# Two-branch decoder layer on one core: compression of keys and values with four products for three output chunks, and the next unit's pages turned inside both halves of the products

## The chip, the cores and the metric

One core of one Trainium2 chip runs the whole kernel as a single program. The metric is the time of one execution on the device in microseconds (us). All data is float32.

## What is computed

The reference is one inference step of a decoder layer for a prompt of 1024 tokens and for 8 decode sequences with 2048 past tokens each. The change touches one stage of it, the compression of the raw keys and values of the past into compressed blocks:

```python
def _compress(kraw, w1, b1, w2, b2, pe):          # CMP_STRIDE = 16, CMP_LEN = 32, CMP_RATIO = 2, CMP_HIDDEN = 256
    ch = kp.reshape(B, n_ch, CMP_STRIDE, NSA_KV_HEADS, HEAD_DIM)
    w1r = w1.reshape(CMP_RATIO, CMP_STRIDE, HEAD_DIM, CMP_HIDDEN)
    parts = jnp.einsum('bnsgd,rsdh->rbngh', ch, w1r)
    n_cmp = n_ch - CMP_RATIO + 1
    h = parts[0, :, 0:n_cmp] + parts[1, :, 1:1 + n_cmp]
    h = h + (pe.reshape(-1) @ w1) + b1
    return jax.nn.gelu(h) @ w2 + b2
```

A sequence of 2048 tokens has 128 chunks of 16 tokens. Output n needs chunk n times the first half of w1 and chunk n + 1 times the second half, so each of the 127 outputs of a sequence and a group of heads is h[n] = A x[n] + B x[n+1], with A and B of 1024 rows (8 tiles of 128) and 256 columns (two halves of 128). It is done for keys and for values, for the prompt (64 chunks) and for 8 sequences, with 2 groups of heads.

## The kernel before

The stage is `compress_and_decode`. The projections of the prompt run ahead of it, the attention of the decode tokens and of the prompt behind it.

**Units and items.** There are NU = 10 units: unit 0 (keys of the prompt), units 1 to 4 (keys of two sequences each), unit 5 (values of the prompt), units 6 to 9 (values of two sequences each). A prompt unit has one item, the others two, one for each sequence. `loads` is the ring of four 1 MB page buffers (`raw0` to `raw3`) that GpSimd fills by indirect DMA in `load`.

**Turning.** `transposes` turns an item's 16 pieces of 128x128 on TensorE into four PSUM banks, by turns in banks 0 to 2 of PS, so a bank can be written when the bank three before it has been read (`bank_free`). ScalarE reads the even banks and VectorE the odd ones (`read_chunks`, with `copy` at L1163), two copies of 64 partitions x 512 for each bank, and puts even and odd chunks apart in the buffer X, which has room for two units.

**Products.** For a pair of outputs the kernel computes three products instead of four: with e and o the even and odd chunks, A (e - o), B (e' - o) and (A + B) o, where e' is the even chunk that follows. The sum A + B is `w1_sum`. GpSimd makes e' - o (`later_difference`, L991), then VectorE makes e - o in place (`first_difference`, L1258). `layer1` runs the products: for each half hh of the hidden columns, 8 matmuls of 256 columns (L1070), 8 of 252 (L1072), and 8 of 256 (L1077). In the trace every one of these float32 matmuls is two weight loads and two MATMUL records. The products of the prompt units are 63 to 65 columns wide.

**Behind the products.** ScalarE copies the shared product to `middle` (L1213), VectorE adds it to the two others (`sums`, L1274 and L1275), ScalarE applies the GELU, and TensorE multiplies with w2 a unit later (`layer2`, L1090 and L1095). Each of the 8 sequence units also does a piece of the layer's modulation: `late_rows` (L1042) multiplies 512 columns of w_ada, ScalarE copies them (L1219), `late_back` (L1049) turns them, and VectorE adds the result to adaT (`late`, L1299) and raises `wa_added`, for which the next `late_rows` waits. The 2 MB of each piece of w_ada are loaded by SyncE once the piece before it is used. In units 1 and 6 `late_rows` stands ahead of the second half, in the others ahead of the first.

**Order of the work.** It is written out by hand. Each engine has one in-order queue, and semaphores join them. TensorE's loop is:

```python
            for u in range(NU):
                if u + 1 < NU:
                    for k in units[u + 1][2]:
                        transposes(pe, items[k])
                layer1(u)
                if u:
                    layer2(u - 1)
                if u in late_at:
                    late_back(late_at.index(u))
```

`layer1(u)` waits for all differences of its unit, then for the `sums` of the same half of unit u - 1. VectorE reads the odd banks of a unit's items, makes the two `first_difference`, and does then `sums` of the unit before. GpSimd, behind the item of unit 5, waits for the end of the products of unit 4 and makes the sum of the value weights (L1004), then goes on with unit 6.

## Time and profile before

| | |
|---|---|
| median of 3 runs | 2244.59 us (2244.12 to 2252.13) |
| the profiled execution, its own time | 2242.59 us |
| its span in the trace | 2240.8 us |
| mean granted TensorE clock, of full speed | 0.978 |
| TensorE busy | 2122.5 us, 95% of the span |
| VectorE, ScalarE, GpSimd busy | 50%, 35%, 40% |
| the stage of the change | from 183.9 us to 452 us of the span |

The span is what the profiler saw between the first and the last instruction, and the execution's own time is 1.8 us longer. PE is TensorE's matmuls, PEld its weight loads, DVE VectorE, ACT ScalarE, POOL GpSimd. Times of rows are counted from the start of the span.

### The profile page before, as it was taken

The numbers are of one execution on the slowest core, as the hardware profiler recorded it, in microseconds if no ns is written. First come the engines' busy times: TensorE is split into PE (matmuls) and PEld (weight loads), VectorE is DVE, ScalarE is ACT, GpSimd is POOL, SyncE is SP. The second block draws the span as 40 slices with busy tenths as digits, with TensorE's granted clock in tenths as the row PEclk, the third lists the DMA queues.
The fourth block names the chain that finished last, engine by engine and source line by source line (L and its number), as shares of the span: only waits on it lengthen the run. The fifth ranks groups of instructions, "written<-read, shape, count | busy, mean of one in ns | idle before, by whom it ended". The sixth has DMA issues, their size and how long they took to land. (4 is left out here: it accounts for less than half of the span.)

```text
span 2240.8 us, 37919 instructions
## 1 busy us (share of the span) xinstructions
PE 2122.5 (95%) x15414; PEld 1875.2 (84%) x15414; DVE 1115.9 (50%) x2002; ACT 791.1 (35%) x1594; POOL 893.2 (40%) x620
## 2 busy tenths in 40 slices
PE   5998999999999989997899999899999999999998
PEld 3997787855777689987799999678999999997886
DVE  5114323254766720259631045666876665664558
ACT  3203222134566621336522131234333333333553
POOL 2322222120111231212321124164388788776786
PEclk8999999998999999998999999999999999999999
DMA  7564434274110051100223130221245344357872
GB/s 265 195 219 153 178 119 150 87 277 167 32 32 11 1 142 38 38 8 3 69 67 95 38 113 20 100 88 65 71 148 178 123 146 165 123 183 272 272 230 104
DMA packets 152757, 268.20 MB, mean 120 GB/s; under 512 B 17817, under 2 KB 86348, under 8 KB 147975
## 3 DMA queue, kind: packets, MB, share of 16 engines
q1 hardware_dynamic: 144375, 222.70, 29.8%
q0 software_dynamic: 8208, 43.07, 5.5%
q8 instruction: 123, 2.02, 0.4%
q14 instruction: 51, 0.41, 0.1%
HBM read 211.93 MB, written 58.08 MB: 120 GB/s over the span
## 5 line engine op out<-in xcount | busy, mean ns | idle before, releaser
L3448 PE MATMUL PS<-down_parts 128*128 128x512 f32 x924 | 213.3, 392 | 0.1
L3448 PEld LDWEIGHTS PS<-down_parts 128*128 128x128 f32 x924 | 174.2, 189 | 38.0 <-issue 0.9
L3405 PE MATMUL PS<-part_hi,w_ring 128*128 128x258 f32 x1152 | 192.2, 285 | 0.0
L3405 PEld LDWEIGHTS PS<-part_hi,w_ring 128*128 128x128 f32 x1152 | 161.8, 191 | 4.6 <-issue 4.6
L3405 PE MATMUL PS<-sum_blocks,w_ring 128*128 128x258 f32 x1296 | 160.1, 284 | 0.9 <-DVE out_sums L3971 0.9
L3405 PEld LDWEIGHTS PS<-sum_blocks,w_ring 128*128 128x128 f32 x1296 | 158.3, 190 | 1.2 <-DVE out_sums L3971 1.2
L643 POOL TENSOR_TENSOR w_merge_parts<-w_merge_raw,w_merge_parts 128x1024 fp32r<-128x1024 f32 x24 | 59.5, 2503 | 202.5 <-ACT w_merge_parts L636 202.5
L3797 POOL TENSOR_TENSOR down_parts<-down_raw,down_parts 128x512 fp32r<-128x512 f32 x71 | 117.4, 1667 | 45.6 <-ACT down_parts L3603 45.2
L2343 PE MATMUL PS<-h_hi,w_merge_parts 128*128 128x344 f32 x768 | 131.4, 323 | 0.0
L2343 PEld LDWEIGHTS PS<-h_hi,w_merge_parts 128*128 128x128 f32 x768 | 122.0, 188 | 3.1 <-issue 3.0
L1809 ACT ACTIVATE scores<-scores,mins_p 128x640 f32<-128x640 f32 (+5 forms) x192 | 112.4, 588 | 28.0 <-DVE mins_p L1851 27.2
L3603 ACT ACTIVATE down_parts<-down_raw 128x1024 fp32r<-128x1024 f32 x77 | 81.6, 1062 | 107.9 <-DMA down_raw<-w_down 61.0
L3405 PE MATMUL PS<-part_lo,w_ring 128*128 128x258 f32 x576 | 117.0, 285 | 0.0
L655 PE MATMUL PS<-h_hi,w_hg_parts 128*128 128x344 f32 x480 | 113.8, 320 | 0.0
L3754 POOL TENSOR_TENSOR w_ring<-w_raw,w_ring 128x512 fp32r<-128x512 f32 x72 | 99.5, 1384 | 32.7 <-ACT w_ring L3586 32.5
L4021 DVE TENSOR_TENSOR down_parts<-down_raw,down_parts 128x512 fp32r<-128x512 f32 x71 | 69.6, 990 | 66.2 <-ACT down_parts L3603 65.9
L1668 POOL TENSOR_TENSOR coef_T<-coef_T 128x128 f32<-128x128 f32 x32 | 14.5, 454 | 206.3 <-DVE coef_T L1895 206.3
L655 PE MATMUL PS<-h_hi,w_merge_parts 128*128 128x344 f32 x384 | 91.2, 320 | 1.6 <-DVE part_lo L2676 1.6
L1736 PE MATMUL PS<-ident,scores 128*128 128x128 f32 x592 | 83.6, 285 | 9.4 <-ACT PT L1784 6.1
L3405 PEld LDWEIGHTS PS<-part_lo,w_ring 128*128 128x128 f32 x576 | 89.8, 191 | 0.0
L3754 POOL TENSOR_TENSOR w_ring<-w_sums,w_ring 128x512 fp32r<-128x512 f32 x54 | 73.0, 1352 | 41.9 <-ACT w_ring L3586 41.9
L1851 DVE CUSTOM_DVE_ANT_0 scores<-PS,toeplitz 128x640 f32<-128x640 f32 (+15 forms) x160 | 77.3, 515 | 17.6 <-PE PS L1718 16.0
(599 smaller groups left out, 5161.3 us busy)
## 6 DMA issues: line engine op xcount, KB each, us to landing
down_raw<-act_blocks SPq DMA_DIRECT2D x77, 256.0 KB, 3.4
w_or_ada<-w_ada SPq DMA_DIRECT2D x8, 2048.0 KB
w_raw<-w_up SPq DMA_DIRECT2D x11, 1024.0 KB, 9.4
w_raw<-w_gate SPq DMA_DIRECT2D x11, 1024.0 KB, 6.7
w_down_rows<-w_down SPq DMA_DIRECT2D x11, 1024.0 KB, 7.3
w_down_blocks<-w_down_sums SPq DMA_DIRECT2D x11, 1024.0 KB, 9.0
down_raw<-w_down_blocks SPq DMA_DIRECT2D x44, 256.0 KB, 4.2
act_blocks<-act_sums SPq DMA_DIRECT2D x10, 1024.0 KB, 5.1
```

Source lines behind the costliest of these rows:

```text
L643: pool.tensor_tensor(r32(self.lo[:, u % 2, k, 0:cols]), self.raw[:, s, :, 0:cols], self.hi[:, u % 2, k, 0:cols], ALU.subtract).then_inc(se ...
L655: last = pe.matmul(out, r32(x), r32(y), start=k + i == 0, stop=k == tiles - 1 and i == 2)
L1736: last = pe.transpose(PS[:, 4 + G % 3, P * k:P * k + P], S[:, n % 2, g, at:at + P], ident[:, :])
L1809: act.activation(S[:, n % 2, g, c:c + cols], S[:, n % 2, g, c:c + cols], ACT.Exp, bias=mn[:, n % 2, x, g:g + 1], scale=-1.0, accum_out=sm[ ...
L1851: return v.tensor_tensor_reduce(S[:, n % 2, g, c:c + cols], src, bias, 1.0, 0.1 * BIG, ALU.add, ALU.min, mn[:, n % 2, x, g:g + 1])
L2343: last = pe.matmul(PS[:, e % RING, 0:W3], r32(left), r32(right), start=p == 0 and k == 0, stop=p == 2 and k == KD - 1)
L3405: last = pe.matmul(out[:, c, :], r32(w[:, k, :]), r32(h[:, k, QUART * c:QUART * c + QUART]), start=first and k + i == 0, stop=k == 3 and i ...
L3448: last = pe.matmul(PS[:, t, c], r32(s[:, x, P * (t % 4):P * (t % 4) + P]), r32(s[:, y, c]), start=first and i == 0, stop=last_j and i == 2 ...
L3603: act.activation(r32(slots[w % 12][:, 0:2, :]), draw[w % 4][:, :, :], ACT.Copy).then_inc(p_hi, 1)
L3754: pool.tensor_tensor(r32(ring[:, (q + 4) % 5, 1]), w_block(u, pos), ring[:, (q + 4) % 5, 0], ALU.subtract).then_inc(w_lo, 1)
L3797: pool.tensor_tensor(r32(s[:, 3, :]), d[:, 1, :], s[:, 1, :], ALU.subtract).then_inc(b_lo, 1)
L4021: v.tensor_tensor(r32(slots[w % 12][:, 2, :]), draw[w % 4][:, 0, :], slots[w % 12][:, 0, :], ALU.subtract).then_inc(a_lo, 1)
```

## The change

**Products.** The 128 chunks of a sequence and group are taken in threes instead of pairs. With d0, d1, d2 the three chunks of a triple and d0' the first of the next, there are TRI = 43 triples, and four products give three outputs. N3 = 4 x 43 = 172 columns for a unit of two sequences and two groups; the product with B has 4 x 42 = 168. For each half there are now 8 matmuls each of 172, 168, 172 and 172 columns, 32 in place of 24. Two of the products need the weights A + B (as before) and A - B (new). The prompt units keep the old scheme.

**Weights.** GpSimd computes A - B for 8 tiles (`subtract_weights`, three instructions over 1, 1 and 6 tiles, 2048 elements per partition in all), once behind the item of unit 0 and once behind the sum of the value weights at unit 5.

**Preparing an item.** A bank is now read with four copies instead of two: for each group one of 4 x 2 x 43 = 344 elements and one of 4 x 42 = 168. GpSimd's difference is over 8 x 2 x 42 = 672 elements (1008 before). VectorE makes three operations over 8 x 86 = 688 elements, each waiting for the one before, where it made one over 1024, and a memset of 16 elements. `first_difference` of each item now comes directly behind its reads, and GpSimd's difference waits for both reads as before.

**Order on TensorE.** The two items of the next unit are not turned ahead of `layer1` any more. The first is turned within the first half, between the second and the third product, and the second at the start of the second half (ahead of `late_rows` in units 1 and 6).

**Behind the products.** `middle` is 344 elements wide, with a scale of 0.5; `sums` is four VectorE operations (one add of 172, then 172, 168, 168) in place of two. SyncE waits also for `summed` and `wa_back` before it loads the window keys, because `middle` and the copy of w_ada's rows now lie in the buffer behind X.

```diff
+TRI = (NCD + 2) // 3
+XN = 8 * 4 * (4 * TRI - 1)
...
+        def subtract_weights(pool, w1):
+            for d, j, n in wdiff:
+                last = pool.tensor_tensor(d[:, :, :], w1[:, j:j + n, :], w1[:, 8 + j:8 + j + n, :], ALU.subtract)
+            last.then_inc(diff_ready, 1)
...
             sp.wait_ge(l1_done, 2 * NU)
+            sp.wait_ge(summed, 2 * NU)
+            sp.wait_ge(wa_back, len(LATE))
...
+                if units[u][1] is not None:
...
+                    pool.tensor_tensor(d, d1[:, :, :, 0:TRI - 1], d0[:, :, :, 1:TRI], ALU.subtract).then_inc(d2_done, 1)
+                    return
...
+                if u == FIRST[0]:
+                    pool.wait_ge(w_in[0], 16)
+                    subtract_weights(pool, wbuf[0])
                 if u == FIRST[1]:
                     pool.wait_ge(w_in[1], 16)
                     pool.wait_ge(l1_done, 2 * (NU // 2))
                     pool.tensor_tensor(wsum[:, :, :], wbuf[1][:, 0:8, :], wbuf[1][:, 8:16, :], ALU.add).then_inc(sum_ready, 1)
+                    subtract_weights(pool, wbuf[1])
...
+            def later_item(u, n):
+
+                if u + 1 < NU:
+                    for k in units[u + 1][2][n:n + 1]:
+                        transposes(pe, items[k])
...
                 for hh in range(2):
                     col = slice(P * hh, P * hh + P)
+                    if hh == 1:
+                        later_item(u, 1)
+                    else:
+                        pe.wait_ge(d1_done, mine[-1] + 1)
+                        pe.wait_ge(d2_done, mine[-1] + 1)
+                        pe.wait_ge(w_in[which], 16)
+                        pe.wait_ge(pe_ready, which + 1)
                     if u in late_at and hh == late_half(u):
                         late_rows(late_at.index(u))
                     if u:
                         pe.wait_ge(summed, 2 * (u - 1) + hh + 1)
...
+                        for j in range(8):
+                            pe.matmul(PS[:, 4 + hh, 0:N3], wt[:, j, col], thirds(u, 0)[:, j, :], start=j == 0, stop=j == 7)
+                        for j in range(8):
+                            pe.matmul(PS[:, 4 + hh, N3:2 * N3 - 4], wt[:, 8 + j, col], thirds(u, 3)[:, j, :], start=j == 0, stop=j == 7)
+                        if hh == 0:
+                            later_item(u, 0)
+                        pe.wait_ge(diff_ready, which + 1)
+                        pe.wait_ge(sum_ready, which + 1)
                         pe.wait_ge(m2_read, 2 * u + hh)
+                        for j in range(8):
+                            pe.matmul(PS[:, 3, 0:N3], wsum[:, j, col], thirds(u, 1)[:, j, :], start=j == 0, stop=j == 7)
+                        for j in range(8):
+                            last = pe.matmul(PS[:, 3, N3:2 * N3], diff(j)[:, col], thirds(u, 2)[:, j, :], start=j == 0, stop=j == 7)
                     last.then_inc(l1_done, 1)
...
             for u in range(NU):
-                if u + 1 < NU:
-                    for k in units[u + 1][2]:
-                        transposes(pe, items[k])
                 layer1(u)
...
+                        for x, nx, nm in ((0, 2, TRI), (2, 1, TRI - 1)):
+                            ins = copy(eng, odd, bass.AP(d.tensor, at + 8 * N3 * x, [list(d.ap[0]), [N3, 4], [8 * N3, nx], [1, nm]]),
+                                       bass.AP(src.tensor, src.offset + x, [list(src.ap[0]), [P, 4], [1, nx], [3, nm]]))
...
+                    own.then(v.memset(d2[:, :, TRI - 1::TRI], 0.0))
+                    v.wait_ge(even_read, read_to(items[k]))
+                    v.wait_ge(d2_done, k + 1)
+                    own(v.tensor_tensor(d0, d0, d2, ALU.subtract))
+                    own.then(v.tensor_tensor(d1, d1, d2, ALU.add))
+                    v.scalar_tensor_tensor(d2, d2, 2.0, d1, ALU.mult, ALU.subtract).then_inc(d1_done, 1)
...
+                    own.then(v.tensor_tensor(both, plus, minus, ALU.add))
+                    v.tensor_tensor(h[:, :, 0::3], PS[:, 4 + hh, 0:N3].rearrange("p (b m) -> p b m", m=TRI), b4, ALU.add)
+                    v.tensor_tensor(h[:, :, 1::3], p4[:, :, 0:TRI - 1], m4[:, :, 0:TRI - 1], ALU.subtract)
+                    v.tensor_tensor(h[:, :, 2::3], b4[:, :, 0:TRI - 1], PS[:, 4 + hh, N3:2 * N3 - 4].rearrange("p (b m) -> p b m", m=TRI - 1),
...
             for k in read_chunks(v, 1, odd_read):
                 u = items[k][0]
+                if u in FIRST:
+                    bias_columns(units[u][0])
+                first_difference(k)
                 if k == units[u][2][-1]:
-                    if u in FIRST:
-                        bias_columns(units[u][0])
-                    for x in units[u][2]:
-                        first_difference(x)
                     if u:
                         for hh in range(2):
                             sums(u - 1, hh)
```

## Rows read from the trace of the kernel before

**Rows 1.** The page, busy us of each engine, share of the span, instructions

```profile
PE 2122.5 (95%) x15414; PEld 1875.2 (84%) x15414; DVE 1115.9 (50%) x2002; ACT 791.1 (35%) x1594; POOL 893.2 (40%) x620
```

**Rows 2.** Timeline of TensorE around unit 7: start us, us, operation, count, idle before

```profile
366.44 1.51 PE L1029 MATMUL PS<-ident,raw 128*128 128x128 f32 x12
...
371.73 1.92 PE L1042 MATMUL PS<-w_or_ada,cT 128*32 128x512 f32 x16
373.59 3.73 PE L1070 MATMUL PS<-XT,w_or_ada 128*128 128x256 f32 x16
377.15 3.56 PE L1072 MATMUL PS<-XT,w_or_ada 128*128 128x252 f32 x16
380.55 3.62 PE L1077 MATMUL PS<-XT,w_sum 128*128 128x256 f32 x16
384.01 3.62 PE L1070 MATMUL PS<-XT,w_or_ada 128*128 128x256 f32 x16
...
394.34 1.88 PE L1095 MATMUL PS<-w,H 128*127 128x64 f32 x16
396.06 1.01 PE L1049 MATMUL PS<-groupsum,ada_rows_late 128*128 128x9 f32 x8
...
427.93 1.92 PE L1042 MATMUL PS<-w_or_ada,cT 128*32 128x512 f32 x16 [0.38 <-DVE adaT L1299]
```

**Rows 3.** Timeline of TensorE, matmuls of other widths and of another kind

```profile
324.71 1.90 PE L1070 MATMUL PS<-XT,w_or_ada 128*128 128x65 f32 x16
...
1118.81 3.95 PE L2343 MATMUL PS<-part_lo,w_merge_parts 128*128 128x344 f32 x24
1122.61 0.60 PE L2401 MATMUL PS<-ident,dec_columns 128*8 128x128 f32 x4
```

**Rows 4.** Groups by line and shape, 184 to 451 us: busy us, mean ns, idle before

```profile
L1163 DVE COPY XT<-PS 64x512 f32<-64x512 f32 x64 | 44.1, 690 | 5.7 <-PE PS L1029 3.9
L991 POOL TENSOR_TENSOR XT<-XT 128x1008 f32<-128x1008 f32 x16 | 40.3, 2519 | 4.8 <-DVE XT L1163 4.6
L1163 ACT ACTIVATE XT<-PS 64x512 f32<-64x512 f32 x64 | 38.2, 597 | 10.6 <-PE PS L1029 9.8
L1258 DVE TENSOR_TENSOR XT<-XT 128x1024 f32<-128x1024 f32 x16 | 19.6, 1226 | 18.1 <-POOL XT L991 17.9
L979 POOL DMA_INDIRECT raw<-cache_cmp_v,cache_rows x8 | 7.6, 951 | 55.1 <-PE PS L1029 54.3 <-issue 0.2
L1163 DVE COPY XT<-PS 64x256 f32<-64x256 f32 x8 | 3.4, 422 | 1.0 <-PE PS L1020 0.9
L1163 ACT ACTIVATE XT<-PS 64x256 f32<-64x256 f32 x8 | 3.1, 386 | 3.2 <-PE PS L1020 3.2
L1258 DVE TENSOR_TENSOR XT<-XT 128x512 f32<-128x512 f32 x2 | 1.4, 692 | 2.3 <-POOL XT L991 2.3
```

**Rows 5.** Timeline of all engines where two items are turned, from 234 us

```profile
234.05 1.51 PE L1029 MATMUL PS<-ident,raw 128*128 128x128 f32 x12
...
234.78 2.43 ACT L1163 ACTIVATE XT<-PS 64x512 f32<-64x512 f32 x4 [0.65 <-PE PS L1029]
235.23 5.75 DVE L1163 COPY XT<-PS 64x512 f32<-64x512 f32 x8 [0.61 <-PE PS L1029]
```

**Rows 6.** Timeline of all engines around the two prompt units

```profile
188.24 0.69 DVE L1258 TENSOR_TENSOR XT<-XT 128x512 f32<-128x512 f32 x1 [1.16 <-POOL XT L991]
...
209.30 3.63 PE L1070 MATMUL PS<-XT,w_or_ada 128*128 128x256 f32 x16
...
317.81 4.54 POOL L1004 TENSOR_TENSOR w_sum<-w_or_ada 128x2048 f32<-128x2048 f32 x1 [19.62 <-PE PS L1077]
...
341.70 3.63 PE L1070 MATMUL PS<-XT,w_or_ada 128*128 128x256 f32 x16
```

**Rows 7.** A long wait of TensorE, then busy us by engine and granted clock

```profile
1445.44 1.63 PE L2847 MATMUL PS<-ident,x_norm 128*128 128x128 f32 x8 [4.75 <-DVE x_norm L3008]
...
1447.00:1449.00 2.00, 2.00 (x6) 1.52 (x5) 0.00 (x0) 0.00 (x0) 0.50 (x1) 0.50 0.64 229
```

More of the change, by code:

```diff
@@ L940, in odds @@
         def odds(u):
-            return X[:, u % 2, 1], shape(u)[1] // 2
+            return pairs(u, 1), shape(u)[1] // 2
         def keys(k):
-            return X[:, k // 2 % 2, k % 2].rearrange("p j n -> p (j n)")[:, 0:STRIDE * P]
+            return cp["keys"][:, k // 2 % 2, k % 2, 0:STRIDE * P]
         @block.sync
@@ L1067, in layer1 @@
                         pe.wait_ge(summed, 2 * (u - 1) + hh + 1)
-                    n1, n3 = 2 * nb * w + first, 2 * nb * (w - 1) + first
-                    for j in range(8):
-                        pe.matmul(PS[:, 4 + hh, 0:n1], wt[:, j, col], X[:, u % 2, 0, j, 0:n1], start=j == 0, stop=j == 7)
-                    for j in range(8):
-                        pe.matmul(PS[:, 4 + hh, M3:M3 + n3], wt[:, 8 + j, col], X[:, u % 2, 2, j, 0:n3], start=j == 0, stop=j == 7)
-                    pe.wait_ge(sum_ready, which + 1)
@@ L1074, in layer1 @@
-                    if u or hh:
+                    if pr is None:
+                        n1, n3 = 2 * nb * w + first, 2 * nb * (w - 1) + first
+                        for j in range(8):
+                            pe.matmul(PS[:, 4 + hh, 0:n1], wt[:, j, col], pairs(u, 0)[:, j, 0:n1], start=j == 0, stop=j == 7)
+                        for j in range(8):
+                            pe.matmul(PS[:, 4 + hh, M3:M3 + n3], wt[:, 8 + j, col], pairs(u, 2)[:, j, 0:n3], start=j == 0, stop=j == 7)
+                        if hh == 0:
+                            later_item(u, 0)
+                        pe.wait_ge(sum_ready, which + 1)
+                        if u or hh:
+                            pe.wait_ge(m2_read, 2 * u + hh)
+                        for j in range(8):
+                            last = pe.matmul(PS[:, 3, 0:2 * nb * w], wsum[:, j, col], pairs(u, 1)[:, j, 0:2 * nb * w], start=j == 0, stop=j == 7)
+                    else:
+                        for j in range(8):
+                            pe.matmul(PS[:, 4 + hh, 0:N3], wt[:, j, col], thirds(u, 0)[:, j, :], start=j == 0, stop=j == 7)
+                        for j in range(8):
+                            pe.matmul(PS[:, 4 + hh, N3:2 * N3 - 4], wt[:, 8 + j, col], thirds(u, 3)[:, j, :], start=j == 0, stop=j == 7)
+                        if hh == 0:
+                            later_item(u, 0)
+                        pe.wait_ge(diff_ready, which + 1)
+                        pe.wait_ge(sum_ready, which + 1)
@@ L1075, in layer1 @@
                         pe.wait_ge(m2_read, 2 * u + hh)
-                    for j in range(8):
-                        last = pe.matmul(PS[:, 3, 0:2 * nb * w], wsum[:, j, col], X[:, u % 2, 1, j, 0:2 * nb * w], start=j == 0, stop=j == 7)
+                        for j in range(8):
+                            pe.matmul(PS[:, 3, 0:N3], wsum[:, j, col], thirds(u, 1)[:, j, :], start=j == 0, stop=j == 7)
+                        for j in range(8):
+                            last = pe.matmul(PS[:, 3, N3:2 * N3], diff(j)[:, col], thirds(u, 2)[:, j, :], start=j == 0, stop=j == 7)
@@ L1176, in read_chunks @@
                             m0 = g * w + odd * w // 2
-                            ins = copy(eng, odd, X[HD * y:HD * y + HD, u % 2, 0:2, :, m0:m0 + w // 2], rows[:, y])
+                            n = 2 * (NCP + 1) + 1
+                            d = X[HD * y:HD * y + HD, u % 2, 0:16 * n].rearrange("p (x j n) -> p x j n", x=2, j=8)
+                            ins = copy(eng, odd, d[:, :, :, m0:m0 + w // 2], rows[:, y])
                     ins.then_inc(done, 1)
```

72 lines of the change are left out of this document (50 added, 22 removed).

## The prediction

> **What bounds the kernel now.** I read the page first: TensorE is busy for 95% of the span and no other engine for more than half of it [rows 1]. A change to the stage is therefore worth what it takes from TensorE's queue there, and nothing else. The timeline of TensorE over the stage comes second. In a unit it goes without a pause from the turning at 366.44 through `late_rows` at 371.73 and the two halves to 394.34, 396.06 and the next turning; what pauses there are lie within the turning [rows 2]. The third view, the groups by line and shape, says why the other engines don't matter today: an odd bank's two copies take VectorE 1.38 us, GpSimd's difference 2.52 us and VectorE's 1.23 us [rows 4], some 10 us of VectorE in a unit that takes 30. All of it is done a whole `layer1` ahead, because both items are turned before the products of the unit before them start. That distance is what the change gives up, so the question is where it leaves no cover. The last view is the timeline around the two prompt units, whose products are short [rows 6].
>
> **The products.** The two widths give the pace. From 373.59 to 377.15, 380.55 and 384.01, 16 records of 252 columns take 3.40 us (213 ns each) and 16 of 256 take 3.46 us (216 ns), the first group after other work 3.56 us [rows 2]. That is 2 cycles of 2.4 GHz for each column and 3 ns. At 65 columns the 16 records take about 1.8 us, 112 ns each, and not 57: there something else, the weight loads by their number, sets a floor [rows 3]. 172 columns by the same slope are 143.3 + 3 = 146.4 ns and lie above that floor; 168 are 143.1 ns. A half is now 16 x (216.4 + 213.1 + 216.4) = 10.33 us, which is what 384.01 to 394.34 shows [rows 2]. It becomes 16 x (3 x 146.4 + 143.1) = 9.32 us. With 16 such halves the gain is 16.3 us. The bounds: without the 3 ns it would be 19 us. From the other side, the nearest records whose columns last 143 ns are the 344-wide ones of L2343, of another kind with one cycle for a column; 24 of them take 3.80 us, 158 ns each [rows 3]. At that pace the 1024 records of the 16 halves would cost 1024 x 12 ns = 12 us more, and the gain would be 4 us. I take 146.4, since the slope between 252 and 256 is that of the very instruction.
>
> **Turning an item.** The fourth bank of an item waits until ScalarE has read its first. ScalarE starts 0.73 us behind the first matmul [rows 5]. Its copies cost 386 ns at 256 elements and 597 at 512 [rows 4], so 458 at 344 and 314 at 168; a bank takes 2 x 0.77 = 1.54 us in place of 1.19. The last four pieces take 0.5 us. An item costs TensorE 0.1 + 0.73 + 1.54 + 0.5 = 2.9 us alone, and two 5.8 us, where two together cost 5.3 us (366.44 to 371.73) [rows 2]. Splitting the turning thus hides none of it, since the queue is in order; it adds 0.5 us to a unit. Going back to products also costs 0.1 us each time (3.56 against 3.46 us [rows 2]), for two breaks in 8 units: 1.6 us.
>
> **The chain behind an item.** VectorE's copies cost 422 ns at 256 and 690 at 512 [rows 4], so 514 and 330 ns; an item's two odd banks take 3.38 us (2.76 before). GpSimd's 672 elements are in proportion 1.68 us. VectorE's differences cost 692 ns at 512 and 1226 at 1024 [rows 4], so 0.88 us at 688; three, each waiting for the last, are 2.7 us. The first copy starts 1.2 us behind the turning [rows 5]. So an item is ready 1.2 + 3.4 + 1.7 + 2.7 = 9.0 us after its turning starts, and two in a row need 7.8 us each, because `first_difference` of the first now stands ahead of the second's copies.
>
> In a sequence unit this is covered. The second item is turned some 7.7 us behind the first, so it is ready about 10.3 us after its turning starts. TensorE meanwhile has 2.9 us of turning, 9.4 of products, 1.7 of `layer2` and 1 of `late_back`, together 15 us. Some 5 us are left; past that, each further us of the chain costs 6 us in all, one for each sequence unit that is prepared behind another.
>
> **At the first prompt unit** it isn't. `layer1(0)` can start when unit 0's difference is done, at 188.24 + 0.69 = 188.9 us [rows 6]. Its first two products take 3.6 us, the turning of unit 1 starts at 192.5 and VectorE's copies at 193.8. Two items in a row end at 193.8 + 2 x 7.8 = 209.4 us, and the prompt's sums (0.6 us, four short operations) at 210.0. TensorE's own work is done by 188.9 + 10.8 + 5.8 + 0.1 = 205.6 us. So `layer1(1)` starts at 210.0 us, 0.7 later than the 209.30 of before [rows 6], with a wait of 4.4 us in front, and before had by then turned unit 2 as well.
>
> **At the second** GpSimd is the late one. It ends the weight sum at 317.81 + 4.54 = 322.35 us [rows 6]. The new subtraction has as many elements (4.7 us with two more starts), the next page's load costs 0.95 us [rows 4], then come the difference (1.7), VectorE (2.7), the second item's copies (3.4), difference (1.7) and VectorE again (2.7), and the sums (0.6): 340.9 us, against 341.70 before. TensorE is free about 337, so it waits some 4 us. Before had by then turned unit 7 too. At unit 0 the same subtraction is hidden: it can run from 188.3 to 193, while nothing waits for GpSimd before 197.
>
> Behind these two points the kernel before still turns four units in pairs (3, 4, 8, 9), 21.2 us; the changed one turns twelve items, 34.8 us. That is 13.6 us more, and 0.7 - 0.8 from the two starts.
>
> **The wait for adaT.** `late_rows` of the next unit now follows `late_back` at once, where a turning lay between. The row at 427.93, the one place where no turning lay between, has TensorE waiting 0.38 us for VectorE [rows 2]; with the restart I take 0.5 us, at five more places (units 1, 2, 3, 6 and 7): 2.5 us. VectorE's two more operations in `sums` are done by then, beside `layer2` and `late_back`. SyncE's two more waits delay loads whose data is wanted 40 us later.
>
> **The clock.** After the 4.75 us wait at 1445.44 the granted clock was 0.50 from 1447 to 1449 us, the 1.2 GHz level [rows 7]. Matmuls at that level take twice as long, and the drop there lasted some 3.4 us, so it costs up to 1.7 us. The changed stage has three such waits: 4 us before 188.9, 4.4 before 210.0, 4 before 341. The bounds are 0 and 5.1 us, or double if a drop lasts twice as long; I take 3.5, as the first lies among short work. The Trainium skill (TensorE: Matmul & The Clock Gate, HAM oscillation) has the clock fall back after each such wait for data; by that rule the three would cost 5.1 us, and the row at 1447 agrees.
>
> **The sum.** -16.3 (products) + 13.6 (turning) - 0.1 (starts) + 1.6 (breaks) + 2.5 (adaT) = +1.3 us, and with the clock +4.8 us. The profiled execution's own time is 2242.6 us, so the changed one is at 2247.4; the median of the runs lies 2.0 us above that execution, so I expect 2249.4 us. A measurement of this kernel can tell a change from none at about 0.5%, 11.2 us: faster is below 2233.4, slower above 2255.8.
>
> **The rivals.**
> (a) The products don't follow the slope. If 172-column records go at the 158 ns of L2343, the time is 2249 + 12 = 2261 us, slower. For it: the 112 ns floor shows that weight loads do matter below some width. Against it: at 252 columns nothing of it is seen. It decides from about 153 ns on.
> (b) The two starts don't wait. If GpSimd and VectorE get through the two chains 4 us sooner, the waits (8 us) and the clock (3.5) go, and the time is 2238 us, still no difference. Against it: both chains are sums of rows, with no slack used.
> (c) The chain outlasts the sequence units too, for instance because the three-element stride of the copies costs more than their count. It needs 5 us more per unit; then 7 us more would give 2249 + 12 = 2261 us. Against it: the copies of before already read with a stride of two at 1.05 ns an element.
> (d) The gain comes through. If in addition to (b) the turning costs no more than before, that is without the 1.54 us wait for ScalarE, the time is 2238 - 6 = 2232 us, faster.
>
> **How the numbers follow.** My forecast, from 2243 (no clock, short restarts) to 2256: 0.60. (a) 0.13, (b) 0.15, (c) 0.07, (d) 0.05. Faster is (d), 0.05; slower is (a), (c), 0.20; the rest, 0.75, is no difference. The range leaves out (d), the lower half of (b) and the upper half of (a) and (c): 2239 to 2260 us. The time is that of the forecast, 2249 us.
>
> **What would show it.** Right: records of 172 columns 146 ns apart and a half of 9.4 us; TensorE waiting 4 us or so ahead of `layer1(1)` and `layer1(6)`, on VectorE; an item turned in 2.9 us; 0.4 us on adaT five more times; a granted clock of 0.50 behind one of the waits; the end of the stage's products within 8 us of before. Wrong: a pace near 158 ns, a wait ahead of `layer1` in units 2 to 4 or 7 to 9, or no wait at the prompt units.

## The result and the profile after

The changed kernel takes 2249.15 us (median of 20 runs, 2243.98 to 2258.14) where the kernel before takes 2245.11 us on the same chips (20 runs, 2239.61 to 2252.13). The ratio is 1.0022, interval 1.0012 to 1.0032: 4.0 us slower by the medians and some 5 us by the ratio, and no difference by the 0.5% that the prediction set. Forecast were 2249.0 us. The profiled execution of the changed kernel is a long one, 2256.87 us, with a span of 2255.1 us against 2240.8 and a mean granted clock of 0.967 against 0.978.

Since one execution varies by more than the change is worth, I read the stage by its own marks: the start of its first turning, `layer1(1)`, `layer1(6)`, and `layer2(8)`, behind which no more products come.

| us | start to `layer1(1)` | to `layer1(6)` | to `layer2(8)` | together |
|---|---|---|---|---|
| before | 25.33 | 132.40 | 108.83 | 266.56 |
| changed | 29.96 | 133.00 | 111.45 | 274.41 |

So 7.9 us of the 14.3 us between the two spans lie in the stage. Its start is 3.4 us later too, in code that both kernels share; over all the profiles below it lies between 183.57 and 188.91 us, whatever the edit, so I don't put it down to the change.

The page's first line, busy us of each engine, answers to [rows 1]. TensorE's busy time is that of before, 2122.8 us, although 16.3 us of products should be gone.

```profile
PE 2122.8 (94%) x15670; PEld 1897.0 (84%) x15670; DVE 1148.5 (51%) x2146; ACT 795.9 (35%) x1658; POOL 887.7 (39%) x626
```

The timeline of TensorE around unit 2, the two starts with a wait, and a half of unit 7 (start us, us, operation, count, idle before):

```profile
192.92 3.68 PE L1120 MATMUL PS<-XT,w_or_ada 128*128 128x65 f32 x16 [4.46 <-DVE XT L1338]
196.39 3.62 PE L1122 MATMUL PS<-XT,w_or_ada 128*128 128x63 f32 x16
199.80 3.62 PE L1069 MATMUL PS<-ident,raw 128*128 128x128 f32 x16
...
217.35 4.60 PE L1132 MATMUL PS<-XT,w_or_ada 128*128 128x172 f32 x16 [3.86 <-DVE H L1366]
...
256.03 1.47 PE L1069 MATMUL PS<-ident,raw 128*128 128x128 f32 x12
258.10 0.66 PE L1069 MATMUL PS<-ident,raw 128*128 128x128 f32 x4 [0.59 <-ACT XT L1226]
258.59 2.50 PE L1141 MATMUL PS<-XT,w_sum 128*128 128x172 f32 x16
260.93 0.75 PE L1143 MATMUL PS<-XT,w_diff 128*128 128x172 f32 x4
...
265.81 2.50 PE L1132 MATMUL PS<-XT,w_or_ada 128*128 128x172 f32 x16
268.15 2.44 PE L1134 MATMUL PS<-XT,w_or_ada 128*128 128x168 f32 x16
270.43 2.50 PE L1141 MATMUL PS<-XT,w_sum 128*128 128x172 f32 x16
272.76 0.75 PE L1143 MATMUL PS<-XT,w_diff 128*128 128x172 f32 x4
273.35 1.91 PE L1143 MATMUL PS<-XT,w_diff_late 128*128 128x172 f32 x12
275.19 1.08 PE L1156 MATMUL PS<-H,w 128*64 128x254 f32 x8
276.20 1.06 PE L1089 MATMUL PS<-groupsum,ada_rows_late 128*128 128x9 f32 x8
277.64 1.92 PE L1082 MATMUL PS<-w_or_ada,cT 128*32 128x512 f32 x16 [0.38 <-DVE adaT L1390]
...
350.35 4.12 PE L1132 MATMUL PS<-XT,w_or_ada 128*128 128x172 f32 x16 [3.75 <-DVE H L1366]
...
396.81 2.50 PE L1132 MATMUL PS<-XT,w_or_ada 128*128 128x172 f32 x16
...
406.10 1.88 PE L1161 MATMUL PS<-w,H 128*127 128x64 f32 x16
```

What to see, beside [rows 2] and [rows 6]: 16 records of 172 columns take 2.34 us (265.81 to 268.15), 146 ns each; a half takes 9.38 us in a unit of the keys (265.81 to 275.19) and 9.29 us in one of the values (396.81 to 406.10), where the kernel before takes 10.42 us (251.62 to 262.04) and 10.33 [rows 2]; an item's turning between two products costs 2.56 us (256.03 to 258.59); the product behind it goes at the same 2.34 us as any other. The wait for adaT is 0.38 us. And the matmuls at 192.92 and 217.35 take nearly twice what the same ones take elsewhere. The wait ahead of `layer1(6)` is 3.75 us at 350.35.

The groups by line and shape over the stage (busy us, mean ns, idle before) answer to [rows 4]:

```profile
L1226 DVE COPY XT<-PS 64x344 f32<-64x344 f32 x64 | 33.0, 515 | 56.7 <-PE PS L1069 55.3
L1021 POOL TENSOR_TENSOR XT<-XT 128x672 f32<-128x672 f32 x16 | 21.8, 1363 | 12.9 <-DVE XT L1226 12.9
L1226 DVE COPY XT<-PS 64x168 f32<-64x168 f32 x64 | 20.7, 323 | 0.0
L1331 DVE TENSOR_TENSOR XT<-XT 128x688 f32<-128x688 f32 x16 | 14.0, 876 | 24.3 <-POOL XT L1021 22.4 <-ACT XT L1226 1.9
L1358 DVE TENSOR_TENSOR middle<-middle 128x172 f32<-128x172 f32 x15 | 9.0, 601 | 43.2 <-ACT middle L1284 43.2
```

Copies and differences are as worked out (515, 323 and 876 ns); GpSimd's 672 elements take 1.36 us and not 1.68. The last row's mean hides one record, which the timeline at the second prompt unit shows (with ScalarE's copies of one item, needed further down):

```profile
327.91 4.33 DVE L1358 TENSOR_TENSOR middle<-middle 128x172 f32<-128x172 f32 x1 [8.03 <-ACT middle L1284]
332.27 0.40 DVE L1359 TENSOR_TENSOR H<-PS,middle 128x172 f32<-128x172 f32 x1
...
333.98 2.64 ACT L1226 ACTIVATE XT<-PS 64x344 f32<-64x344 f32 x8
```

The windows of the stage in which the clock was low (busy us and count of each engine, then the granted clock) are the last view. Before has none between 184 and 451 us.

```profile
190.40:204.10 13.70, 11.18 (x53) 11.08 (x54) 3.47 (x9) 2.61 (x8) 6.84 (x5) 0.51 0.49 195
214.30:221.10 6.80, 3.75 (x13) 3.78 (x14) 3.39 (x11) 2.19 (x4) 0.00 (x0) 0.53 0.00 0
248.50:251.90 3.40, 3.40 (x17) 1.56 (x10) 0.00 (x0) 0.00 (x0) 0.00 (x0) 0.54 0.15 16
350.90:354.30 3.40, 3.40 (x15) 3.40 (x15) 0.84 (x5) 0.40 (x1) 0.00 (x0) 0.54 0.00 0
408.90:412.30 3.40, 3.09 (x16) 0.68 (x16) 0.49 (x2) 0.00 (x0) 0.00 (x0) 0.55 0.00 0
439.60:443.00 3.40, 3.37 (x17) 0.76 (x17) 0.21 (x1) 0.00 (x0) 0.00 (x0) 0.55 0.00 0
```

TensorE is busy for 28.2 us of these (the sum of the second column) at 1.2 GHz, so some 14.1 us of its busy time are the clock's. That is where most of the 16.3 us of products went in the page's first line. Three of the six stretches come with the long waits that the forecast named (4.46, 3.86, 3.75 us), the first two beginning more than 2 us before their wait ends; the other three begin behind waits for adaT of 0.38 us, at 247.82, at 409.21 and at 439.63. The kernel before waits too where the first one stands, for 2.35 us, and its clock stays up:

```profile
190.50 1.06 PE L1029 MATMUL PS<-ident,raw 128*128 128x128 f32 x8 [2.35 <-DVE XT L1163]
```

### The profile page after: what moved, and what is told of

Same layout as the page of the kernel before. It is cut to its first block and busy times, and to the rows that moved or that the text cites. A ratio compares the mean times of both kernels' runs of the same rounds, so it can differ in the third digit from the quotient of the medians.

```text
span 2255.1 us, 38664 instructions
## 1 busy us (share of the span) xinstructions
PE 2122.8 (94%) x15670; PEld 1897.0 (84%) x15670; DVE 1148.5 (51%) x2146; ACT 795.9 (35%) x1658; POOL 887.7 (39%) x626
```

## The experiments

Two theories stood after the result. By the first, the change costs through the places where TensorE now pauses, and mostly through the clock behind them; the products themselves gain what was forecast. By the second, the order costs by its turning (12 items on TensorE's path for 4 pairs) and by its chains, and the clock is a bystander.

### Undoing the order, and the order alone

The changed kernel with both items turned ahead of `layer1`, as before:

```diff
                 for hh in range(2):
...
-                    if hh == 1:
-                        later_item(u, 1)
-                    else:
+                    if hh == 0:
                         pe.wait_ge(d1_done, mine[-1] + 1)
...
-                        if hh == 0:
-                            later_item(u, 0)
...
             for u in range(NU):
+                if u + 1 < NU:
+                    for k in units[u + 1][2]:
+                        transposes(pe, items[k])
                 layer1(u)
```

> The changed kernel with one part undone: both items of the next unit are turned ahead of the products again. Theory (the products gain what their columns say, 16.3 us, and the new place of the turning gives it back): without the wait for adaT (2.5 us), the breaks (1.6) and the turnings that come after the two prompt units (13.6), but with four more copies per item that TensorE waits for (some 0.5 us in each of 8 units) and GpSimd's subtraction still in front of unit 6 (a wait of some 4 us), the median is 2236 to 2241 us, 0.2 to 0.4% below before, and clearly below the changed kernel. Rival (the products or their preparation cost more than their columns say, wherever the turning stands): the median is at 2247 us or above, as with the change.

The other way round, the kernel before with `later_item` at the changed kernel's places and its first differences taken item by item:

> The kernel before with the other part alone: three products for two outputs as before, but the next unit's items turned inside the two halves and each item's difference made behind its own reads. Theory: twelve items turned alone at 2.5 us after the prompt units where four pairs at 5.3 us were turned (+9), starts of the sequence units 6 us earlier in all (-6, the chain of an item is 6.4 us here and GpSimd makes no subtraction), adaT +2.5, breaks +1.6, clock +2: some 9 us above before, 2250 to 2258 us. Rival (the order is harmless and the loss is in the four products): no difference from before, within 2 us.

Measured, beside a kernel before of 2245.14 us: 2243.45 us turned ahead (ratio 0.9985, 0.997 to 0.9999), and 2257.07 us for the order alone (1.0049, 1.0034 to 1.0064). Stages are 261.50 and 282.98 us long. So the order costs 11.9 us with the old products, and the products gain 7.9 us in the new order (2257.07 - 2249.15, beside kernels before of 2245.14 and 2245.11). The second run fell where it should, and it has four stretches at half clock with the old products (13.7, 6.9, 3.4 and 3.4 us), so these belong to the order. That the gain of 7.9 us is half of 16.3 is in part the longer preparation of an item: the changed kernel waits 3.86 and 3.75 us at the two starts where the order alone waits 2.39 and 2.04, its first start is 1.9 us later (29.96 for 28.06 us into the stage), and it has two stretches at half clock more. The first run gained less than the 4 to 9 us expected, and its TensorE timeline says where:

```profile
194.40 3.37 PE L1069 MATMUL PS<-ident,raw 128*128 128x128 f32 x16 [2.90 <-DVE XT L1223]
...
213.85 4.18 PE L1069 MATMUL PS<-ident,raw 128*128 128x128 f32 x20 [4.09 <-ACT XT L1223]
...
326.36 4.25 PE L1069 MATMUL PS<-ident,raw 128*128 128x128 f32 x20 [4.57 <-ACT XT L1223]
```

Turning ahead doesn't remove the waits at the prompt units; they move from the products to the turnings, 11.6 us in three places, and a stretch of 3.4 us at half clock begins at each. In the profiled execution this stage is 5.1 us shorter than before, by the medians the kernel is 1.7; the traces don't show where the rest goes.

### The two sets of pauses, one by one

The changed kernel with the rows of adaT placed behind the second product, so that products lie between `late_back` and the wait:

```diff
-                    if u in late_at and hh == late_half(u):
+                    if u in late_at and hh == late_half(u) == 1:
                         late_rows(late_at.index(u))
...
                             pe.matmul(PS[:, 4 + hh, N3:2 * N3 - 4], ...)
+                        if hh == late_half(u) == 0:
+                            late_rows(late_at.index(u))
```

> The changed kernel, with the product with w_ada of the units that had it ahead of the first half moved behind the second product of that half, so that nobody waits for adaT. Theory (0.4 us of waiting and 0.1 us of restart at six places): 2.5 to 3 us less than the changed kernel. Second theory, from the trace after: the granted clock fell to 0.5 behind three of these places, at 248.5, 408.9 and 439.6 us, and each fall cost 1.7 us; if the short stretch of small work with a wait at its end is what lets it fall, the gain is up to 8 us. Rival (the wait is only moved to another place): no difference.

And the changed kernel with TensorE turning the identity while it would wait, into a bank that nobody reads:

```diff
+                        if u in (0, 1, 6):
+                            if u == 6:
+                                pe.wait_ge(wa_added, 4)
+                            for _ in range({0: 30, 1: 32, 6: 28}[u]):
+                                pe.transpose(PS[:, 7, 0:P], ident[:, :], ident[:, :])
                         pe.wait_ge(d1_done, mine[-1] + 1)
```

> The changed kernel with TensorE turning the identity matrix into a spare bank 30, 32 and 28 times (3.6 to 4.1 us) in the waits ahead of the products of units 0, 1 and 6; nothing else is changed, and no other engine waits for it. Theory (the waits also cost clock): the granted clock stays at 1.0 behind 190, 214 and 350 us, and the time falls by 3 to 7 us. Rival (the waits cost their own length alone): no difference, or up to 1 us slower where the fill outlasts a wait.

Measured: 2245.19 us (0.9993, 0.998 to 1.0007) and 2240.29 us (0.9971, 0.9958 to 0.9985), that is 4.0 and 8.9 us under the changed kernel. The first keeps the stretches at half clock behind the three long waits and loses all three behind adaT; its stage is 266.45 us. The second is the test of the clock: it adds 90 matmuls and takes nothing away, and it gains more than the 3 to 7 us expected; its stage is 263.21 us. TensorE at unit 0:

```profile
186.47 3.44 PE L1113 MATMUL PS<-ident 128*128 128x128 f32 x30
191.10 2.00 PE L1125 MATMUL PS<-XT,w_or_ada 128*128 128x65 f32 x16 [1.19 <-DVE XT L1343]
192.94 1.95 PE L1127 MATMUL PS<-XT,w_or_ada 128*128 128x63 f32 x16
```

The 65-column product takes 2.00 us in place of 3.68. This run's stage shows one stretch at half clock, at 426.6 us. That decides for the first theory as far as the clock goes: the fills can shorten nothing but what the clock costs. That the turning costs too holds beside it, as the sum below has it. Both edits together:

> The changed kernel with two edits that were each run alone: the rows of adaT of units 2, 3, 4, 7, 8 and 9 placed behind the second product, and 30, 32 and 28 turnings of ident ahead of the waits in front of the first product of units 0, 1 and 6. Theory (the change's own cost is half clock after short waits, in two separate sets of places): the two gains, 4.0 and 8.9 us, touch different records and add: 2236, between 2234 and 2239, and the trace shows no stretch at half clock between 184 and 455 us. Rival (the clock falls somewhere else instead, as the fourth run of the first batch showed at 426.6 us): 2240 to 2243, with one or two stretches at half clock left.

Measured, beside a kernel before of 2244.82 us: 2238.47 us (0.9963, 0.9949 to 0.9976), faster than before and than the changed kernel, and inside what was expected. The gain against the changed kernel is 10.4 us by the two differences to before (-6.35 and +4.04), where the two alone would add to 12.9. One reason may be that the fills alone already show one stretch behind adaT and not three, but which of these places has one changes from profile to profile, and 2.5 us are within the intervals. The windows of its stage, with the granted clock in the third column from the end, and its two starts:

```profile
184.00:210.00 26.00, 22.82 (x200) 21.91 (x201) 15.51 (x39) 7.60 (x22) 12.32 (x9) 1.00 0.57 203
210.00:338.00 128.00, 121.70 (x909) 110.08 (x908) 64.62 (x151) 35.71 (x94) 29.82 (x21) 1.00 0.42 149
338.00:443.00 105.00, 101.03 (x735) 92.78 (x735) 44.55 (x111) 26.45 (x69) 13.87 (x12) 1.00 0.37 127
```

```profile
183.92 1.07 PE L1060 MATMUL PS<-ident,kv 128*128 128x128 f32 x8 [1.46 <-PEq L703]
...
209.71 2.57 PE L1137 MATMUL PS<-XT,w_or_ada 128*128 128x172 f32 x16 [0.92 <-DVE H L1373]
...
337.83 2.57 PE L1137 MATMUL PS<-XT,w_or_ada 128*128 128x172 f32 x16 [0.50 <-DVE H L1373]
...
443.15 1.88 PE L1168 MATMUL PS<-w,H 128*127 128x64 f32 x16
```

Its stage is 259.23 us long, in parts 25.79, 128.12 and 105.32. This is the change at full clock and without the adaT waits: 7.3 us shorter than before, and 15.2 us shorter than the changed kernel's. The edit has a price of its own, 0.16 us at six places for two more breaks around `late_rows` (2.38 us for 2.28 ahead of it, a turning of 2.62 for 2.56 behind). The run is also the control for the chains: with the clock out of the way `layer1(1)` starts 25.79 us after the stage, 0.5 us later than before, where the prediction had 0.7.

The same help for the kernel that turns ahead, with the turnings of the identity ahead of its three waits:

> The changed products with both items turned ahead of the products as before the change, and 24, 32 and 34 turnings of ident ahead of the waits of 2.9, 4.1 and 4.6 us in which that order's turnings of units 1, 2 and 6 stand. Theory (three stretches of 3.4 us at half clock, each some 1.7 us of TensorE's time, follow those waits): 5 us less than without them, 2238.4, between 2236 and 2240, not better than the split order with the same help. Rival (the waits themselves, 11.6 us together, are what costs, and turning in them is no help): 2243 to 2244, as without it.

Measured: 2245.65 us (0.9995, 0.9979 to 1.0011), no gain, and outside both what the theory and what the rival had. It tells less than it should, because the edit carried a wait of its own: TensorE has to be sure of the bank at unit 5 and stands there for adaT, [4.02 <-DVE adaT] ahead of the 34 turnings, with a stretch of 6.8 us at half clock. At the first two places the half clock is gone, and `layer1(1)` still starts 29.91 us into the stage, 0.75 us sooner than the same order's 30.66, so there the wait was mostly the chain. Whether that order could be brought to 2238 us too is open.

### VectorE beside the weight sum

The record of 4.33 us above is 13 times its usual 0.34 us. It starts 0.4 us behind GpSimd's weight sum (327.53, 4.51 us) and ends 0.2 us behind it. The Trainium skill (SBUF — State Buffer, SBUF: two separate sides) says that a VectorE instruction with two inputs in SBUF and a GpSimd instruction that reads SBUF exclude each other for the whole instruction, the later one waiting; this trace agrees, with 4.33 us for 0.34. I had priced `sums` without it. Five runs tried to take it away or moved it. First in the order that turns ahead, with the sum in eight instructions, and then with the weight subtraction behind the second item's difference of units 1 and 6 as well:

```diff
-                    pool.tensor_tensor(wsum[:, :, :], wbuf[1][:, 0:8, :], wbuf[1][:, 8:16, :], ALU.add).then_inc(sum_ready, 1)
+                    for j in range(8):
+                        last = pool.tensor_tensor(wsum[:, j:j + 1, :], ...)
+                    last.then_inc(sum_ready, 1)
```

> The kernel of e1_turn_ahead with GpSimd's sum of the value weights (2048 elements, one instruction of 4.51 us) done as 8 instructions of 256. In e1_turn_ahead VectorE's add of 172 elements, both inputs in SBUF, took 4.33 us beside that sum instead of 0.34, ScalarE's GELU and reads came behind it, and TensorE waited 4.57 us at 326.36. Theory (the two engines exclude each other for a whole instruction): the add takes at most 1 us, TensorE's wait there falls to about 0.6 us, the clock stays up at 326.7, and the time is 4 to 6 us below e1_turn_ahead: 2238 to 2240 us where before is at 2245. Rival (the add waits for something else, its semaphore for instance): the row stays at 4.3 us and the time doesn't move.

> f1_ahead_sum_pieces with GpSimd's subtraction of the weights (5 us each) moved behind its difference for the second item of unit 1 and of unit 6, so that it doesn't stand ahead of those items. Theory (GpSimd's queue is what makes the items of the first sequence units late): TensorE's waits for VectorE's reads and for the bank of unit 2 (2.9 and 4.1 us in e1_turn_ahead, at 194.4 and 213.85) shrink by some 4 us together, and the clock drops there with them: 2232 to 2237 us. Rival (VectorE's own chain of reads and three operations sets that time): within 1 us of f1.

Measured, beside a kernel before of 2246.02 us: 2246.34 us (0.9998, 0.9985 to 1.0011) and 2240.91 us (0.9985, 0.9969 to 1.0001). Both missed their ranges, the second by less. Their stages are 264.15 and 264.65 us, so the two profiles don't show where the 5.4 us between the medians come from. In pieces the sum lets VectorE in (its addition takes 0.54 us), but takes 5.72 us itself, and the wait comes back one unit later: 6.04 us at 342.76, ahead of unit 7's turning. There ScalarE waits for VectorE's `sums(5)`, which stand in VectorE's queue behind unit 6's differences, which wait for GpSimd. With the subtraction moved, it meets the three differences of the next item. VectorE and GpSimd of that run at 201 to 209 us:

```profile
202.65 1.27 DVE L1330 TENSOR_TENSOR XT<-XT 128x688 f32<-128x688 f32 x1 [1.50 <-POOL XT L1021]
203.85 1.40 DVE L1331 TENSOR_TENSOR XT<-XT 128x688 f32<-128x688 f32 x1
205.28 3.99 DVE L1332 SCALAR_TENSOR_TENSOR XT<-XT 128x688 f32<-128x688 f32 x1
```

```profile
202.47 2.04 POOL L959 TENSOR_TENSOR w_diff<-w_or_ada 128x256 f32<-128x256 f32 x2
204.48 4.06 POOL L959 TENSOR_TENSOR w_diff_late<-w_or_ada 128x1536 f32<-128x1536 f32 x1
```

Three instructions of 0.88 us take 6.7 us together. In the split order, with all four edits:

> The changed kernel, turning split as in it, with all mends together: the product with w_ada later (e3), the waits ahead of units 0, 1 and 6 filled with 32, 36 and 16 turnings of the identity (e4), the weight sum in pieces, and the subtraction behind the second item. Theory: e4 was 8.9 us below the changed kernel; the wait for adaT takes 3 us more away and the shorter chain at unit 6 another 1.5: 2234 to 2237 us. Against f2: if the split turning is worse for its own sake (2.9 us an item with nothing hidden), f2 is faster than this by 0 to 5 us; if it is as good, they are equal.

Measured: 2248.99 us (1.0008, 0.9993 to 1.0022), a clear miss, by the same meeting (3.98 us at 210.07): the waits ahead of `layer1(1)` and `layer1(6)` are 4.50 and 5.45 us behind turnings that were to fill them, each with 6.8 us at half clock. In the split order the place that the changed kernel gives the subtraction is the better one: the next run has all of this but the late subtraction (and 30, 32 and 28 turnings for 32, 36 and 16), and takes 2240.12 us. In the order that turns ahead the medians say the opposite (2240.91 us late, 2246.34 early), and why is open. The sum alone in pieces, on the best kernel so far:

> The run before it with the weight sum of the value stage in eight GpSimd instructions of an eighth each. Theory (VectorE's addition of the two products waited for the one long GpSimd instruction): the addition takes 0.5 us in place of 4.3, the wait of the first turning of unit 6 falls from 1.0 to 0.6 us, and the time is up to 3 us shorter, 2234 to 2236. Rival (the chain is then set by GpSimd itself: eight pieces took 5.72 us in place of 4.51 in an earlier run, and the subtraction behind them ends as much later): the addition is short, but the wait ahead of the first product of unit 6 stays or grows by 1.2 us: 2236 to 2239. Before the run the rival is the likelier, since the same edit on the kernel that turns ahead moved the wait and lost 2.9 us.

Measured: 2240.12 us (0.9967, 0.9952 to 0.9982), 1.65 us above the run beside it, with intervals that overlap. What speaks is the trace: from `layer1(1)` to `layer1(6)` it takes 129.19 us (210.05 to 339.24) against 128.12: GpSimd's chain is longer by about what the eight instructions cost, as the rival said, though the time lies above the rival's range as well. The wait ahead of `layer1(6)` is 2.00 us in place of 0.50, and a stretch of 3.4 us at half clock begins at 340.4. So at the second prompt unit the 4.33 us of VectorE were mostly covered, and what decides is, by this reading, GpSimd's own weight work (9.5 us, 327.53 to 337.00 in the changed kernel). The last run of this kind makes the sum wait for VectorE in the order that turns ahead:

> The changed products, both items turned ahead as before, and GpSimd's weight sum of the value stage waits until VectorE has made the sums of unit 4 (one more wait on GpSimd; the sum starts 1.6 us later and ends 1.6 us later). Theory (the 4.57 us wait ahead of unit 6's turning and the stretch at half clock behind it come from VectorE's addition, locked out for 4.33 us by that sum): the addition takes 0.34 us, the wait falls to about 0.6 us, no half clock at 326; 4.0 + 1.7 us less than the 2243.5 of the same kernel without it: 2238, between 2236 and 2241. Rival (GpSimd's chain is what is late, and it gets later): the wait comes back ahead of unit 7's turning or products, as it did with the sum in pieces: 2243 to 2246.

Measured, beside a kernel before of 2244.61 us: 2243.65 us (0.9994, 0.998 to 1.0008). The addition takes 0.34 us and the wait at unit 6's turning is gone, but the timeline has it at unit 7's, as the rival said:

```profile
344.40 4.71 PE L1070 MATMUL PS<-ident,raw 128*128 128x128 f32 x20 [6.74 <-ACT XT L1224]
```

What is excluded from beside the sum was asked by one run with a copy in front of the addition:

```diff
+                    if u == 4 and hh == 1:
+                        own.then(v.tensor_scalar(both, plus, 1.0, None, ALU.mult))
                     own.then(v.tensor_tensor(both, plus, minus, ALU.add))
```

> The changed kernel with one more VectorE operation at unit 4's second half, just ahead of the addition of the two products: it writes 1.0 times one of them (128 x 172, one input from SBUF, result to SBUF) to the addition's own target. It stands beside GpSimd's weight sum as the addition did. Theory (VectorE and GpSimd lock each other out only where VectorE has two inputs in SBUF): the copy takes about 0.2 to 0.3 us in the middle of the sum, and the addition behind it takes what is left of the sum, about 4 us. Rival (SBUF is slow for all of VectorE beside that sum, or VectorE's first operation after a long wait is what is slow): the copy takes the 4 us and the addition 0.34. The time is within 1 us of the changed kernel's, of which one execution tells nothing.

```profile
323.54 4.24 DVE L1359 TENSOR_SCALAR middle<-middle 128x172 f32<-128x172 f32 x1 [8.02 <-ACT middle L1284]
327.81 0.74 DVE L1360 TENSOR_TENSOR middle<-middle 128x172 f32<-128x172 f32 x1
...
330.11 1.53 DVE L1226 COPY XT<-PS 64x344 f32<-64x344 f32 x4
```

```profile
323.16 4.51 POOL L1043 TENSOR_TENSOR w_sum<-w_or_ada 128x2048 f32<-128x2048 f32 x1 [10.87 <-PE PS L1143]
...
329.11 3.53 POOL L959 TENSOR_TENSOR w_diff_late<-w_or_ada 128x1536 f32<-128x1536 f32 x1
```

My theory, as I had narrowed it to two inputs, fell: the copy, with one input, took the 4.24 us (one execution, 2250.89 us). What the same profile shows unharmed is the copies out of PSUM at 330.11: beside GpSimd's subtraction the four take the 1.53 us that they take elsewhere. The same page of the Trainium skill (SBUF — State Buffer, Who interferes with whom) has a VectorE instruction shut out too if it runs in a mode that uses both ports, and names `tensor_scalar` among those that can, on conditions for their operands. The 4.24 us fit that, but would fit a general hold on SBUF to SBUF work as well, and no run here tells the two apart.

## Why the prediction came out

The time was 2249.15 us where 2249.0 stood, inside 2243 to 2256, and no difference at 0.5%. That is closer than the working deserves: turning and breaks stood 5.7 us too high and the clock between 4 and 5 us too low, and that the two errors cancel is luck.

**Products, -16.3.** Held. 146 ns a record; a half is 1.04 us shorter, like compared with like (10.42 to 9.38 for keys, 10.33 to 9.29 for values), so 16 x 1.04 = 16.7 us. Rival (a), the pace of 158 ns, is out.

**Turning, +13.6.** Too high. An item costs 2.56 us, not 2.9: 12 x 2.56 - 21.2 = 9.5 us. The step that failed is "a bank takes 2 x 0.77". It added two durations of ScalarE that overlap; eight copies of a turned item lie in 2.64 us by the timeline, while their durations sum to 4 x (457 + 293) = 3.0 us. In its place the fourth bank begins 2.07 us behind the first (256.03 to 258.10), where the forecast has 0.1 + 0.73 + 1.54 = 2.37. "It adds 0.5 us to a unit" fell with it: two items turned apart cost 5.1 us, less than the 5.3 of a pair before, and than the 5.5 of a pair with the new copies (370.40 to 375.93 in the run that turns ahead). The loss is in how many items are left to turn behind the two starts, not in splitting them.

**Breaks, +1.6.** Nothing: the product behind a turning goes at the pace of any other (258.59 to 260.93).

**Starts, -0.1.** The mechanism held, and at full clock the sizes nearly so, by the run with both edits: `layer1(1)` 0.5 us late for 0.7. The stretch up to `layer1(6)` is 4.3 us shorter than before; by the measured terms its eight halves gain 8 x 1.04 = 8.3 us, its turning loses 6 x 2.56 - 2 x 5.3 = 4.8, and that run's own breaks 3 x 0.16 = 0.5, which leaves 3.0. So the start itself is some 1.2 us early, where 0.8 stood. With the clock down it was otherwise: 4.6 us late at `layer1(1)`. The prediction worked that start out by the chain at full clock, and added the clock as if the two were apart. The drop of 13.7 us lies on the turning of unit 1, with which the chain begins, so it delays it. That kind of drop is no accident of one execution: the three other profiles of the split order without fills have it at the same place (13.6 or 13.7 us).

**adaT, +2.5.** Held. The wait is 0.38 us and with its restart 0.52 us: from `late_back` to the next matmul it is 1.44 us (276.20 to 277.64), and 0.92 us where nothing is waited for (264.50 to 265.42 in the run with both edits). Five more places are 2.6 us. But the forecast didn't see that the clock falls there as well, at three of the six.

**The clock, +3.5.** This is the term that was mis-sized, and the one that makes the change a loss. The stage without it and without the adaT waits is 7.3 us shorter than before; with them 7.9 us longer. Of those 15.2 us adaT's six waits are 3.1, and the run without them had 1.0 us of breaks that the changed kernel hasn't, so the clock is some 13 us in the profiled execution. That fits the 28.2 us of busy time at half clock. By the medians, which average over what the clock did in other executions, the 15.2 us are 10.4 and the clock so some 8. The bounds that I gave, 0 and 5.1 us or double "if a drop lasts twice as long", took [rows 7] as the length of every drop. Here one lasted 13.7 us, where short products and turnings follow, and one 6.8 us, where products of 172 columns do; at that second place two later profiles of the split order (the rows of adaT later, the copy ahead of the addition) show 3.4 us, and the order alone 6.9. I doubled nothing because the one row that I had showed 3.4 us. The Trainium skill (TensorE: Matmul & The Clock Gate, HAM oscillation) has the clock fall after each such wait; the trace agrees for the three long ones, and the price that I worked out for that rule, 5.1 us, was too low as well.

**The sum.** With the measured sizes: -16.7 + 9.5 + 0 + (0.5 - 1.2) + 2.6 = -5.3 us. With the clock's 13 that is +7.7 in the profiled stage, which measures +7.9; with 8 it is +2.7, where the medians say +4.0. The forecast had +1.3 and +3.5. Rival (b), waits that don't come, is out, and so is (c): there is no wait ahead of `layer1` in units 2 to 4 or 7 to 9. The kernel with both edits has the time that (b) names, 2238 us, by another road: the waits are filled and not gone. (d), 2232 us, is reached by no run.

Not forecast at all was that VectorE's additions meet GpSimd's weight sum (4.33 us). In the split order it cost TensorE the 0.4 us by which one wait at unit 6's turning is longer (1.01 for 0.59), so it didn't move the result. It would have moved rival (b).

## What to carry to other kernels

When a change opens a pause on the engine that bounds the kernel, price what the clock does around it apart from the pause, and with the bound of a long drop where short work follows (13.7 us here, in four profiles, where the row at hand had 3.4). Here the help given to nine pauses of 0.4 to 4.5 us was worth 10.4 us, more than the 7.3 us that the change gains in its stage without them. If such a pause can't be removed, idle matmuls in it can be worth more than the change itself (8.9 us here, for 90 of them), and a short wait is best moved behind work that is ready anyway. When a long GpSimd instruction is added or moved, look what VectorE does from SBUF to SBUF beside it, and don't add up durations of records that overlap: take the time from first to last of a group.

## What the runs showed of the hardware

- A pause of 0.38 us between `late_back` and `late_rows` was followed by half clock at three of six places in the changed kernel (247.82, 409.21, 439.63 and not at 277.64, 305.82 or 380.46), at two with one VectorE copy more (243.44, 376.30), and at one each with the waits filled (426.61) and with the order alone (246.91). With products in place of the pause it was at none. What tells the places apart is not settled, and since they change with edits elsewhere, one profile doesn't show it.
- Nor does the length of a longer wait alone decide: 2.35 us in the kernel before (190.50) left the clock up, 2.04 us with the order alone (353.00) did not.
- Around a wait of 4.46 us the granted clock was 0.51 for 13.7 us, although TensorE was busy without a pause for the last 11.2 of them, with matmuls of 63 to 65 columns and turnings.
- Beside a GpSimd sum of 4.51 us, VectorE's 128 x 172 addition took 4.33 us for 0.34, and a one-input copy 4.24 us; copies from PSUM beside a GpSimd subtraction took no longer (1.53 us for four). One of three 688-element operations took 3.99 us for 0.88.
- The same GpSimd sum in eight instructions took 5.70 to 5.72 us for 4.51, 0.17 us for each more.
